# Head-pair walk of the bidirectional SSD layer: each direction's decay matrix multiplied by x on its own and added in PSUM, in place of one addition by VectorE

## What is computed

```python
seg = jnp.exp(jnp.where(lower, a_t[..., :, None] - a_t[..., None, :], -jnp.inf))
cb = jnp.einsum("bclgn,bcsgn->bcgls", cm, bm)
y_diag = jnp.einsum("bcgrls,bcsgrp->bclgrp", cb[:, :, :, None] * seg, xs)
...
y_off = jnp.einsum("bclgn,bcgrpn->bclgrp", cm, h_start) * jnp.exp(a_cs)[..., None]
return (y_diag + y_off), h_last
...
for k, rev in ((0, False), (1, True)):      # both directions, outputs added
    ...
    yl = yl + y_l
    yc = yc + y_c
```

## Time and profile before

| | |
|---|---|
| median of three runs | 1607.54 us (1605.97 to 1609.85) |
| the profiled execution | 1607.82 us, of which the span from its first to its last instruction is 1606.1 us |
| TensorE (PE) busy | 1346.7 us, 84% of the span |
| VectorE (DVE) busy | 541.1 us, 34% |
| ScalarE (ACT) busy | 374.8 us, 23% |
| GpSimd (POOL) busy | 221.7 us, 14% |
| mean granted TensorE clock | 0.914 |
| the walk, first to last `outputs` | 184.1 to 493.2 us of the span |

### The profile page before, as it was taken

One profiled execution on the slowest core, in us unless ns is written; L12 is line 12 of the kernel. 1 busy time (PEld: TensorE's weight loads), 2 busy tenths in 40 slices (PEclk: granted clock), 3 DMA queues, 4 the chain that ended last, 5 costly groups with the idle time before them and its releaser, 6 DMA issues.

```text
span 1606.1 us, 12860 instructions
## 1 busy us (share of the span) xinstructions
PE 1346.7 (84%) x4984; PEld 624.6 (39%) x4984; DVE 541.1 (34%) x762; ACT 374.8 (23%) x703; POOL 221.7 (14%) x211
## 2 busy tenths in 40 slices
PE   2499999999999992699999945999888739899873
PEld 0244444444444442344333422444445424333221
DVE  0356466666651415011111125442373321111102
ACT  0225566666660100000000002100442100000000
POOL 0101233443341001200000012120000010000000
PEclk9699999999999995799999977999786759999997
DMA  9224466666576035469999978200004518799994
GB/s 347 101 61 152 181 226 232 216 240 213 207 269 253 27 118 223 152 211 421 427 430 427 426 266 290 88 0 0 13 1 171 211 41 307 296 428 426 429 428 195
DMA packets 78629, 367.38 MB, mean 229 GB/s; under 512 B 7905, under 2 KB 26273, under 8 KB 63201
## 3 DMA queue, kind: packets, MB, share of 16 engines
q1 hardware_dynamic: 67067, 331.39, 52.9%
q0 software_dynamic: 5408, 17.91, 3.2%
q10 hardware_dynamic: 6092, 17.24, 2.7%
HBM read 350.49 MB, written 16.02 MB: 228 GB/s over the span
## 4 chain that ended last, share of the span: by engine, by line
PE 67%; DMA 16%; DVE 7%; issue 3%; SPq 2%; ACT 2%; POOL 1%; ACTq 0%; DVEq 0%; POOLq 0%
PE psum L1386 22%; PE psum L676 9%; PE psum L1735 8%; PE psum L687 7%; DMA ring<-in_moe_w_up 6%; PE psum L1021 5%; DMA ring<-in_moe_w_down 4%; PE psum L282 2%; PE psum L1759 2%; PE psum L1805 2%; DMA ring<-in_moe_w_gate 2%; DMA arena<-mod_d 1%; PE psum L720 1%; PE psum L740 1%; PE psum L1778 1%
## 5 line engine op out<-in xcount | busy, mean ns | idle before, releaser
L1386 PE MATMUL psum<-ring,arena 128*64 128x512 f32 (+1 forms) x1536 | 492.4, 613 | 37.6 <-DMA ring<-in_moe_w_gate 11.6
L1386 PEld LDWEIGHTS psum<-ring,arena 128*64 128x64 f32 (+1 forms) x1536 | 182.9, 161 | 329.3 <-issue 272.9
L676 PE MATMUL psum<-hT,ring 128*128 128x512 f32 x384 | 169.5, 596 | 0.0
L1735 PE MATMUL psum<-ring,hT 128*128 128x512 f32 x320 | 141.6, 606 | 6.9 <-ACT arena L1816 6.9
L1021 PE MATMUL psum<-ring 128*128 128x512 f32 x256 | 113.4, 601 | 3.3 <-DVE X L1071 2.0
L687 PE MATMUL psum<-hT,ring 128*128 128x512 f32 x256 | 112.5, 592 | 0.0
L676 PEld LDWEIGHTS psum<-hT,ring 128*128 128x128 f32 x384 | 71.4, 190 | 91.8 <-issue 91.8
L1735 PEld LDWEIGHTS psum<-ring,hT 128*128 128x128 f32 x320 | 62.2, 195 | 85.2 <-issue 85.2
L881 DVE SCALAR_TENSOR_TENSOR arena<-arena,cols 128x512 f32<-128x512 f32 x96 | 92.8, 966 | 3.4
L1460 ACT ACTIVATE arena<-psum 128x512 f32<-128x512 f32 x22 | 13.1, 597 | 323.2 <-PE psum L1386 323.2
L1486 DVE TENSOR_TENSOR arena<-arena,psum 128x512 f32<-128x512 f32 x22 | 23.0, 1046 | 159.3 <-PE psum L1386 159.3
(11 more groups left out here) (251 smaller groups left out, 1432.7 us busy)
## 6 DMA issues: line engine op xcount, KB each, us to landing
ring<-in_moe_w_gate SPq DMA_DIRECT2D x32, 2048.0 KB, 21.2
ring<-in_moe_w_up SPq DMA_DIRECT2D x32, 2048.0 KB, 19.7
ring<-in_moe_w_down SPq DMA_DIRECT2D x32, 2048.0 KB, 19.5
arena<-in_ada_w SPq DMA_DIRECT2D x60, 512.0 KB, 6.3
ring<-in_ssd_w_in SPq DMA_DIRECT2D x16, 1024.0 KB, 6.9
ring<-acs_d SPq DMA_DIRECT2D x16, 1024.0 KB, 7.0
ring<-in_da_w_in SPq DMA_DIRECT2D x6, 2048.0 KB, 18.9
moe_y_d<-arena ACTq DMA_DIRECT2D x22, 512.0 KB, 10.3
```

The costliest lines, as they stand in the source:

```text
L676: mm = pe.matmul(psum[:, bank, :], w_[:, k, c0:c0 + P], hT[:, k, :], start=(k == 0), stop=(k == KD - 1))
L1386: mm = pe.matmul(psum[rows, dst, :], lhsT[:, k, rows], slot(s_, a)[:, k, part], start=(k == 0), stop=(k == a - 1))
L1735: mm = pe.matmul(psum[:, 4 + m_ % 2, :], hT[:, k, t * P:(t + 1) * P], slot(qkv_slot[n], KD)[:, k, :], start=(k == 0), stop=(k == KD - 1))
```

## The change

`outputs` multiplies both directions' G by the same x, and lets PSUM add them: the first direction's matmul starts the accumulation, the second adds. `decay_vector` no longer adds, and signals `g_ready` from the multiplication.

```diff
             for c_ in range(TT):
                 dst = psum[:, 5 + i % 2, c_ * P:(c_ + 1) * P]
-                for hh in range(2):
-                    r = slice(64 * hh, 64 * hh + 64)
-                    pe.matmul(dst[r, :], xtok[:, i % 2, c_, r], E[i % 2][:, 2 * c_, hh * P:(hh + 1) * P], start=True, stop=False)
+                for d_ in range(2):
+                    for hh in range(2):
+                        r = slice(64 * hh, 64 * hh + 64)
+                        pe.matmul(dst[r, :], xtok[:, i % 2, c_, r], E[i % 2][:, 2 * c_ + d_, hh * P:(hh + 1) * P], start=(d_ == 0), stop=False)
                 for last, (d_, n, lv) in enumerate(OFFS[c_], 1):
...
-            step(v.tensor_tensor(out=e4, in0=e4, in1=cb, op=ALU.mult))
-            e2 = E[i % 2].rearrange("p (c d) b -> p c d b", d=2)
-            v.tensor_tensor(out=e2[:, :, 0, :], in0=e2[:, :, 0, :], in1=e2[:, :, 1, :], op=ALU.add).then_inc(g_ready, 1)
+            v.tensor_tensor(out=e4, in0=e4, in1=cb, op=ALU.mult).then_inc(g_ready, 1)
```

## The result

The changed kernel takes 1620.17 us (median of 4 runs, 1619.99 to 1621.01) where the kernel before, on the same chips, took 1606.76 (4 runs, 1598.92 to 1609.85). The ratio is 1.0092, with a 95% interval of 1.0056 to 1.0128: slower, by some 9 to 21 us (13.4 us between the medians). The profiled execution is 1620.04 us against 1607.82, 12.2 us more. The prediction was 1620.7, or 13.1 more.

What follows compares the result with a forecast made beforehand. TensorE's full instruction list bounds the walk over head pairs (first to last `outputs`, 309.06 us). Added matmuls 14.0 less 0.9 of stall gives +13.1: 1620.9 from the profiled 1607.8, put at 1620.7 us from the median; range 1617.5 to 1624.

Steps and rivals of the forecast that it cites:

- The added pairs: TensorE in `outputs`: 4 more matmul pairs a step, 64 in 16 steps, at 0.218 us each, adding 13.95 us.
- Rival (a): `outputs`: an added pair's heads don't run side by side, or its second direction waits; +27.5 us, about 1634; 4 in 100.
- The removed addition: VectorE in `decay_vector`: one 1.226 us addition a head pair goes, 19.6 us of work; 16.4 us of slack, gain 0.
- Rival (b): VectorE's addition paces the `outputs` steps through `g_ready`; removal returns 19.6 against 14.0 added, -5.6, about 1602; 2 in 100.
- (c): Hidden TensorE idle time between first and last `outputs` absorbs part of the added work; about +10, 1617.5; 7 in 100.
- The one stall: TensorE's 1.76 us wait for an adaLN piece's DMA absorbs one step's growth and shrinks to 0.89; 0.87 us back.
- After the walk: The 1113 us after the last `outputs` contain neither touched step and only move as a whole; cost 0.
- The sum of 13.1: Whole kernel: 14.0 us for added matmuls less 0.9 for TensorE's shrinking DMA wait, +13.1 on the profiled 1607.8 us.
- Rival (d): Behind the last `outputs`, DMAs land otherwise or the clock falls elsewhere; +3 us or more, 1624 and up; 5 in 100.

Runs made afterwards that it cites:

- the third pair: The changed kernel with direction 1's pair of matmuls standing twice in each chunk; 1633.54 us, ratio 1.0192 to the kernel before.

## Why the prediction was right, and where it was wrong

**The added pairs: right.** 64 at 0.218 us, 13.95 predicted, 13.98 measured as busy time in the walk, 14.03 for the next 64. Rival (a), 27.5 us, is out, by the groups of eight and the third pair. The Trainium skill's 81 ns for a matmul of 128 columns (TensorE: Matmul & The Clock Gate, Back-to-back issue gap) gave estimates of 10.4 or 20.7 us; the measurement is neither, 55 ns an entry with two side by side.

**The removed addition: right.** Nothing gained, shown by the kernel without it at 309.08 us. Rival (b) falls with it, and (c) by the plain period, which grew by the full 0.87 us. One argument against (c) was weak: a period that repeats to 0.01 us doesn't show that nobody waits. With ten additions, where TensorE waits, the periods repeat as well (30.80, 34.94, 29.16 us, three times within 0.01). My reason for it was only half right: 16.4 us of slack to `g_ready` is the wrong measure for how free VectorE is. The nearer deadline is `gated_vector` behind the addition on the same queue, with 4.6 us, which the prediction worked out and did not use as the bound. Five additions in place of one break it. One sign came out otherwise too: `gated_vector` doesn't start at once behind line 903, but waits 1.62 us for `outputs`. In the step shown VectorE reaches that line 0.58 us before `outputs` starts (314.80, 315.38), where it was 1.18 behind (312.18, 311.00), since line 915 before it is shorter now. The slack of `tokens_T` did grow by some 2 us (from 4.6 to 6.7).

**The one stall: wrong in sign.** The step that failed is "So its landing does not move with the `outputs(13)` that now is 0.87 us longer: that step's growth falls into the stall, which shrinks to 0.89." The issue did not move, but the landing did, by 1.5 us, since with the longer instruction list an instruction fetch fell into that load and held up its last packets on one DMA engine. The prediction's own bounds, 0 to 1.76 us given back, left out that the stall could grow. -0.87 predicted, +0.61 measured, and +2.2 where the clock fell too. With the fetch moved away the step is right to 0.2 us (1.05).

**After the walk: right as far as it can be told.** The rest was 1111.51 us against 1112.94; the kernel before again has 1111.51, and over the eleven profiles without a third pair or further additions this stretch lies between 1104 and 1117 us, and the one ahead of the walk between 183.0 and 184.9. So the profiled difference of 12.2 us is 14.6 in the walk less 2.3 of such scatter (0.86 ahead of it, 1.43 behind). The sum of 13.1 came closer to 12.2 than its terms deserve: the stall's error of 1.5 us and the scatter of 2.3 had opposite signs. That 1620.7 met the median of 1620.17 so closely is luck in part as well: it was built on a median of 1607.54 for the kernel before, whose later medians were 1602.41 to 1605.55, and the changed kernel's second median was 1618.11. What the medians can tell is 13.4 and 14.5 us more, each with some 6 us to either side. Rival (d) has nothing for it.

## What to carry to other kernels

Where one engine's list is the length of a stage, an operation moved onto it costs its full issue distance, here 0.218 us times 64, and what it relieved on a half-idle engine was worth nothing; accumulating in PSUM was free only for the engine that no longer adds. Read the price from the distance between starts where the same pattern already stands, and read the slack of a relieved engine from everything queued behind the removed instruction, not only from its own signal. A term under 1 us that rests on one DMA's landing should be carried with both signs.

## What the runs showed of the hardware that I had not expected

- One 16 KB instruction fetch inside the 1 MB load of a piece sits on one of the 16 DMA engines for 0.97 us, the piece's packets behind it wait, and the load lands 1.5 us later (6.1 in place of 4.6 us). Adding instructions anywhere ahead moves where the fetch falls: 160 more (40 matmuls of four each) moved it from 3.9 us behind the load's issue to 12.5 us ahead of it.
- The same wait of TensorE in the same kernel, 2.37 and 2.32 us, was followed once by a granted clock of 1.00 and once by 0.50 for some 3 us, worth 1.6 us.
- The two heads' matmuls share the array also when each head's two directions stand together in the list: 22.07 against 22.02 us a period.
